# Earlier row sums and difference rows for a three-group fast product, and two reorderings inside units of the attention heads

## What is computed

```python
x = x + o @ w_out                        # end of layer 2: chunks 32 to 35
h = rms_norm(x, pre_norm_w)
proj = h @ w_in                          # 2048 x 5952
sb_q, sb_k, sb_v, sb_gate, c_q, c_kv, k_rope, mla_gate = split(proj)
q_full = rms_norm(c_q) @ w_q_up          # then rope on 64 of 192 per head
kv     = rms_norm(c_kv) @ w_kv_up
p = softmax(mask(q_mla @ k_mla.T))       # per head, chunk-causal
```

## Time and profile before

| what | us |
|---|---|
| median of 3 runs (lowest, highest) | 1261.71 (1261.41, 1262.15) |
| the profiled execution's own time | 1261.45 |
| its span in the trace | 1259.7 |
| PE busy in the span | 1245.4 |
| DVE busy | 890.2 |
| ACT busy | 792.7 |

### The profile page before, as it was taken

How to read it: one execution, slowest core, us unless ns; L and a number is a source line. 1 busy time by engine, 2 the same in 40 slices (tenths; PEclk the granted TensorE clock), 3 DMA queues, 4 the chain that set the end, 5 groups by cost and what they waited for, 6 DMA issues and landing times.

```text
span 1259.7 us, 16169 instructions
## 1 busy us (share of the span) xinstructions
PE 1245.4 (99%) x5897; PEld 1035.5 (82%) x5897; DVE 890.2 (71%) x1411; ACT 792.7 (63%) x1241; POOL 204.9 (16%) x149
## 2 busy tenths in 40 slices
PE   9999999999999999999999999998999999999998
PEld 7888888888888888888888888887988788888886
DVE  5497898476657667888777765658587767576545
ACT  5798798765547556655567774456655455666543
POOL 1499999900000000000000000000000000000000
PEclk9999999999999999999999999999999999999999
DMA  9899999944565565666555446565655556655563
GB/s 348 269 256 251 269 255 242 269 164 142 181 195 184 186 187 180 201 199 203 167 155 162 154 148 203 185 174 157 187 167 167 163 157 194 192 164 157 182 196 134
DMA packets 133566, 243.86 MB, mean 194 GB/s; under 512 B 12144, under 2 KB 22512, under 8 KB 133360
## 3 DMA queue, kind: packets, MB, share of 16 engines
q1 hardware_dynamic: 129600, 229.40, 58.7%
q0 software_dynamic: 3600, 13.11, 5.3%
q10 hardware_dynamic: 288, 0.32, 0.1%
HBM read 227.60 MB, written 2.10 MB: 182 GB/s over the span
## 4 chain that ended last, share of the span: by engine, by line
PE 94%; DVE 3%; ACT 1%; issue 0%; DMA 0%; DVEq 0%; SPq 0%; ACTq 0%
PE PS L1928 27%; PE PS L1930 27%; PE PS L1929 27%; PE PS L1839 2%; PE PS L1966 2%; PE PS L1968 2%; PE PS L1967 2%; PE PS L1858 1%; PE PS L2127 1%; DVE w_lo L1199 1%; PE PS L2023 0%; PE PS L2025 0%; PE PS L2024 0%; ACT w_hi L685 0%; DMA w_raw<-in_a_w_in 0%
## 5 line engine op out<-in xcount | busy, mean ns | idle before, releaser
L685 ACT ACTIVATE w_hi<-w_raw 128x1024 fp32r<-128x1024 f32 (+2 forms) x383 | 395.7, 1037 | 339.2 <-PE PS L1930 298.4
L1199 DVE TENSOR_TENSOR w_lo<-w_raw,w_hi 128x1024 fp32r<-128x1024 f32 (+2 forms) x339 | 403.4, 1193 | 252.5 <-ACT w_hi L685 251.8
L1928 PE MATMUL PS<-w_hi,actA_hi 128*128 128x512 f32 x736 | 288.9, 393 | 0.9 <-DVE w_lo L1199 0.9
L1930 PE MATMUL PS<-w_hi,actA_lo 128*128 128x512 f32 x736 | 286.9, 390 | 0.0
L1929 PE MATMUL PS<-w_lo,actA_hi 128*128 128x512 f32 x736 | 286.5, 389 | 0.0
L1928 PE MATMUL PS<-w_hi,actB_hi 128*128 128x512 f32 (+1 forms) x646 | 255.5, 396 | 2.0 <-DVE w_lo L1199 2.0
L1930 PE MATMUL PS<-w_hi,actB_lo 128*128 128x512 f32 (+1 forms) x646 | 249.6, 386 | 0.0
L1929 PE MATMUL PS<-w_lo,actB_hi 128*128 128x512 f32 (+1 forms) x646 | 249.0, 385 | 0.0
L1928 PEld LDWEIGHTS PS<-w_hi,actA_hi 128*128 128x128 f32 x736 | 138.1, 188 | 29.9 <-issue 2.0
L1930 PEld LDWEIGHTS PS<-w_hi,actA_lo 128*128 128x128 f32 x736 | 138.1, 188 | 29.4
L1929 PEld LDWEIGHTS PS<-w_lo,actA_hi 128*128 128x128 f32 x736 | 138.2, 188 | 28.2
(11 more groups left out here) (386 smaller groups left out, 1479.8 us busy)
## 6 DMA issues: line engine op xcount, KB each, us to landing
w_raw<-in_a_w_in SPq DMA_DIRECT2D x95, 512.0 KB, 5.8
w_raw<-in_w_in SPq DMA_DIRECT2D x88, 512.0 KB, 3.7
w_raw<-in_w_kv SPq DMA_DIRECT2D x64, 512.0 KB, 3.8
w_raw<-in_b_w_in SPq DMA_DIRECT2D x64, 512.0 KB, 3.8
w_raw<-in_a_w_out SPq DMA_DIRECT2D x32, 512.0 KB, 3.7
w_raw<-in_b_w_out SPq DMA_DIRECT2D x32, 512.0 KB, 3.7
w_raw<-in_w_out SPq DMA_DIRECT2D x32, 512.0 KB, 4.2
tap_products<-tap_products POOLq DMA_DIRECT2D x25, 512.0 KB, 8.4
```

The source lines that it names most:

```text
L685: nc.scalar.activation(split_slot(u)[0][:, f:2 * w], w_raw[:, RAW_SLOT[u], f:2 * w], ACT.Copy)\
L1199: V.tensor_tensor(wl, w_raw[:, RAW_SLOT[u], f:2 * w], wh.bitcast(F32), ALU.subtract)\
L1928: T.matmul(bank, ah, wh[:, kk, :], start=(first or opens_last and tok == 1) and kk == 0, stop=False)
L1930: ins = T.matmul(bank, al, wh[:, kk, :], start=False, stop=last and kk == 1)
```

## The change

Five edits. (1) `late_acts` runs at units 276, 277, 278 and 293 in place of 291, 292, 293 and 295; its high part on ACT at 291 in place of 294. (2) `late_differences` is done in two parts: k tiles 4 to 11 at units 283, 284, 285 and 287 (ACT 286), k tiles 12 to 15 at 291, 291, 292 and 296 (ACT 293), in place of 297, 298, 299 and 301 (ACT 300) for all; the second operand lies at another place in `aux`. (3) On ACT the copies of turned sb_q and sb_k stand ahead of a head's exponentials and of the sums' high parts. (4) On DVE a head's division by its sums is issued at the end of its first unit instead of the head of the second. (5) `differences` is cut in two, its last two operations after that division.

```diff
-LATE_ACTS_AT, LATE_DIFF_AT = DONE[C_CQ - 1] + 3, DONE[C_CQ - 1] + 9
+LATE_ACTS_AT = [DONE[C_OUTB + 1] + at for at in (4, 5, 6)] + [DONE[C_OUTB + 3] + 5]
+LATE_DIFF_AT = [[DONE[C_OUTB + 2] + at for at in (3, 4, 5, 7)], [DONE[C_OUTB + 3] + at for at in (3, 3, 4, 8)]]
...
+                for i, (m, dst, scale) in enumerate((("sq", sq_t, float(DH ** -0.5)), ("sk", sk_t, 1.0))):
+                    for j in range(2):
+                        if u == FIRST[LATE[i + 1]["c"]] + 2 + j:
+                            copy_pairs(f"{m}{j}", lambda b: dst[:, 4 * j + 2 * b:4 * j + 2 * b + 2, :], scale,
+                                       LATE[i]["col2"])
                 if u + 2 in SEVEN_AT:
...
-                if u == LATE_ACTS_AT + 3:
+                if u == LATE_ACTS_AT[3] - 2:
                     act.wait_ge(S["late_acts"], 1)
                     chunk_done(act, C_CQ - 1)
...
-                if u == LATE_DIFF_AT + 3:
-                    act.wait_ge(S["late_diff"], 1)
...
+                for i in range(2):
+                    if u == LATE_DIFF_AT[i][2] + 1:
+                        act.wait_ge(S["late_diff"], i + 1)
+                        part = late_diffs(0)[i]
+                        nc.scalar.activation(part, aux[:, 4 * H8:4 * H8 + part.shape[-1]], ACT.Copy)\
+                            .then_inc(S["late_diff_hi"], 1)
...
-            def differences(u):
+            def differences(u, half):
...
+                if half == 0:
+                    for v in (u, u + 1):
+                        dve.wait_ge(S[f"w{RAW_SLOT[v]}_loaded"], RAW_LOADED[v])
+                    if n >= 2:
+                        dve.wait_ge(S["units_done"], [v for v in SEVEN_AT][n - 2] + 2)
+                    V.tensor_tensor(t1_t3, w_raw[:, at + 1, :].rearrange("p (m n) -> p m n", m=2),
+                                    w_raw[:, at:at + 2, 0:NC], ALU.subtract).then_inc(S["sums_made"], 1)
+                else:
+                    dve.wait_ge(S["sums_made"], 2 * n + 1)
+                    link(V.tensor_tensor(t2, b22, t1_t3[:, 0, :], ALU.subtract))
+                    V.tensor_tensor(t4, b21, t2, ALU.subtract).then_inc(S["sums_made"], 1)
...
-                    dve.wait_ge(S["lo_ready"], LO_NO["v3"] + 1)
+                    dve.wait_ge(S["lo_ready"], LO_NO["v1"] + 1)
...
+            def late_differences(i, step):
+
+                k0, k1 = (12, KT) if i else (LATE_PLAIN, 12)
+                d, rest = (aux[:, at:at + P * (k1 - k0)].rearrange("p (k n) -> p k n", n=P) for at in (4 * H8, 0))
+                if step < 2:
+                    part = (lo if step else hi)["B"][:, k0:k1, :].bitcast(F32)
+                    dve.wait_ge(S["lo_ready"], LO_NO["v3" if i else "v2"] + 1)
+                    link(V.tensor_tensor(rest if step else d, part[:, :, 0:P], part[:, :, P:SEQ], ALU.subtract))
...
-                    if b == 1:
-                        m = h % 2
-                        dve.wait_ge(S["m_exp"], h + 1)
...
                 if u + 3 in SEVEN_AT:
-                    differences(u + 3)
+                    differences(u + 3, 0)
                 if u + 2 in SEVEN_AT:
                     differences_lo(u + 2, 0)
                 if u + 1 in SEVEN_AT:
                     differences_lo(u + 1, 1)
+                h, b = divmod(u - MLA_FROM, MLA_STEP)
+                if 0 <= h < HEADS and b == 0:
+                    m = h % 2
+                    dve.wait_ge(S["m_exp"], h + 1)
+                    link(V.reciprocal(recips[:, 0:2], sums[:, 0:2]))
...
+                if u + 3 in SEVEN_AT:
+                    differences(u + 3, 1)
...
-                    pe.wait_ge(S["late_diff_lo"], 1)
+                    pe.wait_ge(S["late_diff_lo"], 2)
```

More of the change, by code:

```diff
@@ L461, in late_diffs @@
         def late_diffs(lo_part):
[L462 to L465, removed]
+            at, n = 4 * NC + 512 * LATE_SUMS, (12 - LATE_PLAIN) * P
+            return [aux_r[:, 6 * H8 + lo_part * n:6 * H8 + (lo_part + 1) * n],
+                    flat_a(lo if lo_part else hi)[:, at:at + 4 * P]]
         def late_diff(lo_part, k):
-            d = k - LATE_PLAIN
-            return late_diffs(lo_part)[d // 8][:, d % 8 * P:(d % 8 + 1) * P]
+            d = k - 12 if k >= 12 else k - LATE_PLAIN
+            return late_diffs(lo_part)[k >= 12][:, d * P:(d + 1) * P]
         def late_join(g, half, tok):
@@ L1209, in differences @@
                 assert RAW_SLOT[u + 1] == at + 1
[L1210 to L1213, removed]
                 b21, b22 = w_raw[:, at, NC:2 * NC], w_raw[:, at + 1, NC:2 * NC]
@@ L1289, in late_acts @@
                     V.tensor_tensor(s4, a12, s2, ALU.subtract).then_inc(S["late_acts"], 1)
-                if step == 4:
+                if step == 3:
                     dve.wait_ge(S["late_acts_hi"], 1)
@@ L1306, in late_differences @@
                     V.tensor_tensor(d, d, rest, ALU.add).then_inc(S["late_diff"], 1)
[L1307 to L1315, removed]
+                if step == 3:
+                    dve.wait_ge(S["late_diff_hi"], i + 1)
+                    part, part_hi = (late_diffs(n)[i] for n in (1, 0))
+                    V.tensor_tensor(part, aux[:, 4 * H8:4 * H8 + P * (k1 - k0)], part_hi.bitcast(F32), ALU.subtract)\
+                        .then_inc(S["late_diff_lo"], 1)
             def join_late(n, g):
@@ L1568, in _ @@
                             .then_inc(S["d_pt_lo"], 1)
-                h, b = divmod(u - MLA_FROM, MLA_STEP)
-                if 0 <= h < HEADS:
-                    if b == 1:
-                        m = h % 2
-                        dve.wait_ge(S["m_exp"], h + 1)
[L1575 to L1579, removed]
                 h, b = divmod(u - SB_FROM, SB_STEP)
@@ L1613, in _ @@
                         .then_inc(S["m_negmax"], 1)
-                late_acts(u - LATE_ACTS_AT)
-                late_differences(u - LATE_DIFF_AT)
+                for step, at in enumerate(LATE_ACTS_AT):
+                    if u == at:
+                        late_acts(step)
+                for i in range(2):
+                    for step, at in enumerate(LATE_DIFF_AT[i]):
+                        if u == at:
+                            late_differences(i, step)
                 for n in range(2):
@@ L1626, in _ @@
                     differences_lo(u + 1, 1)
+                h, b = divmod(u - MLA_FROM, MLA_STEP)
[3 more added lines that the diff above has]
+                    link(V.reciprocal(recips[:, 0:2], sums[:, 0:2]))
+                    for tok, (f, e) in enumerate(((0, 128), (128, 384))):
+                        ins = V.tensor_scalar(work[:, m, f:e], work[:, m, f:e], recips[:, tok:tok + 1],
+                                              None, ALU.mult)
+                    ins.then_inc(S["m_probs"], 1)
+                if u + 3 in SEVEN_AT:
+                    differences(u + 3, 1)
                 if u == SQUARES_AT[1]:
```

5 lines of the change are left out of this document (removed).

## The result

The changed kernel takes 1254.97 us (median of 4 executions, 1254.60 to 1255.28) against 1261.70 for the kernel before on the same chip (1261.41 to 1262.15): 6.73 us less, ratio 0.9946, 95% interval 0.9929 to 0.9963. Forecast were 1255.8 with a range from 1254.9 and a chance of 0.89 for faster by over 0.2%. The direction and the mechanism came as written; the time lies at the lower edge of the range, and by the ratio to the kernel before (1261.71 x 0.9946 = 1254.897) a hair under it. So there is a missed term to be found: 6.7 instead of 5.9.

The account below looks back on a forecast made before the run. TensorE bounds the kernel, busy 1245.4 of 1259.7 us. Gains 4.16 + 0.45 + 0.97 = 5.58, with 0.3 for restarts 5.9, took 1261.45 to 1255.6; 0.26 to the median gave 1255.8, range 1254.9 to 1258.2.

Parts of the forecast that it names:

- Units 300 to 304: End of the c_kv projection: three PE stalls of 0.93, 2.19 and 1.04 us would go, 4.16 us gained.
- the slower first matmuls: First matmul after each PE wait takes some 0.08 us longer; 0.3 us more gained for four waits.
- The cover: Units 276 to 296: 11.6 us of work moved onto VectorE hides in its idle time and slack, cost 0.
- The 0.45 of three more instructions: VectorE's moved work: three cuts at 0.15 us each add 0.45 us by the skill's rule; nothing charged, as VectorE idles there.
- Heads: Units 332 and 337: earlier copies of turned chunks gain 0.45 us, probabilities ahead of weight differences gain 0.97 us.
- the carry from one execution to the median: Profiled execution of 1261.45 us less 5.9 gives 1255.6; the median lies 0.26 above it, so 1255.8.
- the low end of the range: Given as 1254.9 us: the forecast less 0.3 for restarts counted double and 0.7 for the spread of runs.
- B: Units 304 to 309: thin margins in the VectorE and ScalarE chain give half of 4.16 back, 1257.9 us; chance 0.15.
- C: Units 294 to 296: crowding on ScalarE holds low weights, 4.5 us given back, 1260.3 us; chance 0.06.
- D: Units 276 to 296: VectorE is not truly idle, all 11.6 us exposed, 1267.4 us; chance 0.04.
- E: The move does nothing since the new rows wait for their sources anyway; ruled out, no chance of its own.

Follow-up runs that it names:

- e7: The kernel before run again with no edit: 1261.97 us against 1261.96, ratio 1.0000.
- e9: The changed kernel run again, unchanged: 1255.61 us against 1262.25 for the kernel before, ratio 0.9947.
- e5: The changed kernel with two unused additions of 1536 elements on VectorE in unit 291: 1257.71 us against 1261.96 for the kernel before, ratio 0.9967.
- e6: The changed kernel with four more additions of 1536 elements on VectorE in unit 284: 1262.10 us against 1261.96 for the kernel before, ratio 1.0004.
- e3: The kernel before with only the row sums moved: 1261.85 us against 1262.08, ratio 1.0000.
- e4: The kernel before with only the difference rows moved, kept at another place in the buffer: 1259.47 us against 1262.08, ratio 0.9981.
- e1: The kernel before with row sums and difference rows moved, heads left as they were: 1256.77 us against 1262.08, ratio 0.9958.
- e2: The kernel before with only the three edits of the heads, rows as before: 1260.74 us against 1262.08, ratio 0.9990.
- e8: The changed kernel with two more orders turned round, on ScalarE and VectorE: 1254.61 us against 1261.96 for the kernel before, ratio 0.9943.
- e10: The kernel of e8 run again beside e9: 1254.69 us against 1262.25 for the kernel before, ratio 0.9940.

## Why the prediction was right in kind and short in size

**Units 300 to 304, 4.16.** Right, and a little small. All three stalls went (4.18 by the steps), and no wait came in their place. The stretch is 4.67 shorter, 4.49 between e7 and e9. The 0.5 on top: 0.22 for the slower first matmuls behind the three, which I had in the sum; a stall of unit 302 that the list doesn't show, and that I had overlooked in the trace of before, 0.15 at 871.95 and 0.08 behind it; and the rest in gaps under 0.05.

```profile
871.65 0.31 PE L1930 MATMUL PS<-w_hi,actB_lo 128*128 128x320 f32 x1
871.95 0.38 PE L1928 MATMUL PS<-w_hi,actB_hi 128*128 128x320 f32 x1
```

**The cover, cost 0.** Right, and shown by e5 and e6: 1.84 of room in the crowded place (2.1 said), 2.9 in the quiet one (3.4 said). The working was 0.3 to 0.5 too generous. The 0.45 of three more instructions stayed hidden (DVE's busy time rose by 0.6, 890.2 to 890.8), so here the trace sides against charging for the rule of the Trainium skill ("VectorE: DVE Perf Modes", "Rules for kernel authors").

**The part that I costed without its partner.** I wrote of the row sums only that their new place costs nothing. e3 and e4 show that they win nothing alone and 1.86 as room for the difference rows. That is no error of the sum, but the prediction didn't say it, and my expectation of e4 was wrong by it: I followed the late weights only to unit 295 and left out what the row sums' high and low parts meet in the short units behind.

**Heads, 0.45 + 0.97.** Right: 1.48 in the table. e1, without the three edits, keeps the stretch as long as before's; e2, with them alone, has it 1.49 shorter.

**The step that failed: the carry from one execution to the median, and the low end of the range.** The sum was made against one execution (1261.45) and carried to the median with a fixed 0.26. The median came 0.83 under the forecast. Of that 0.25 are the two stretches (6.15 in place of 5.9, and 0.23 of it the stall at 871.95), 0.45 the first 211 units, 0.04 the part behind unit 349, and 0.11 that the changed kernel's profiled execution lay 0.15 under its median and not 0.26; the rest is rounding. Between profiles the first 211 units, the same in all but for edit 5, ended between 595.68 and 596.66, a spread of 0.98, and the changed kernel's first profile was the earliest of the twelve, with e1 0.01 behind. That the scatter fell that way was chance: in e9 the same kernel came 0.76 later. What makes this scatter is open. The low end had too little room for it: I gave 0.7, the spread of the kernel before's three executions, as if only one of two kernels scattered, and nothing for a stall that I hadn't found. The subtraction was also wrong: 1255.8 less 0.3 less 0.7 is 1254.8, not 1254.9; 1254.8 would have held the result, by luck and not by a better term.

**The clock, a term that the prediction hasn't.** In two of the four profiles that kept the wait of 2.04 us (before, e2, e3, e7) the clock fell behind it, for 0.33 and 0.57 us. In the seven profiles whose PE waits stay under 2 us (after, e1, e4, e5, e8, e9, e10) it didn't fall in these units. How often it falls in the timed executions can be judged by their mean granted clocks. The profiles with a fall have 0.997 and 0.998, before and e7 have 0.999. Of the 37 executions of the changed kernel, e1, e4, e5, e8, e9 and e10, 36 have 0.999 or 1.000. Of the 63 of the kernel before in the later comparisons (without the one of 2083.73), 36 have 0.998 or less, with a median of 1262.26, and 27 have 0.999, with a median of 1261.73. So about half of its executions seem to pay some 0.5 us that the changed kernel doesn't; where in them the clock fell wasn't recorded, and one execution of e2 has 0.949 at an ordinary 1261.83, so a single entry proves little. It is of the right size for the second comparison: against the four executions beside e9 that have 0.999 (median 1261.68) e9 gains 6.07, and the stretches of e7 and e9 say 6.01. In the first comparison only the profiled execution's clock is on record, 0.999, and the kernel before's 1261.70 is no higher than that of the 27; there the 0.45 of the early part is the larger share of the excess, and the clock's share stays open.

**Rivals.** B did not come: PE had no wait in units 304 to 309, though e4 and e5 show that the place exists. C and D did not come. E was rightly excluded: the first of the moved operations (805.61) starts right behind the low part in front of it.

## What to carry to other kernels

Work off the critical engine has a right place: put it where the critical engine's steps are long (units of 512 columns, 2.72 us) and not where they are short (320 columns, 1.76 us), and check the crowded iterations by a forward working with the wanted time beside each step. Moves come in sets: one that is worth nothing alone can be what makes room for the other. A wait of the matrix engine can cost more than its length, since the clock may fall behind it; where such a wait is removed, count that on the side of the gain.

## What the runs showed of the hardware

Behind idle time of PE of 2.04 us the granted clock fell to 0.57 in e2 and to 0.54 in e3 (means of 2 us), and did not in the profile of before or in e7; behind 4.04 us it fell to 0.50 (e6), behind 1.54 us it did not (e5). From 880 us (e2, e3) and 842 us (e6) it was 0.97 to 1.00 again. Matmuls were 0.27 apart for 320 columns and 0.43 for 512 in the meantime, against 0.147 and 0.23. Additions chained by a semaphore on DVE took 7.13 us for four of 1.75, and 3.54 for two, so some 0.04 a link.
